# Hymba encoder: order of the fillings beside the HGRN scan

## Reference

```
h = rms_norm(x, norm1_w);  u = h @ w_in
y_a = rwkv7_mixer(shifted part of u)          # (T, 512)
y_b = hgrn2_mixer(u): chunked scan, both directions, o = o_fwd + o_bwd
      o = o * rsqrt(mean(o*o per head) + eps) * gnorm_w * silu(gate)   # (T, 512)
x  = x + concat(y_a, y_b) @ w_out
h2 = rms_norm(x, norm2_w)
group = argmax(h2 @ wg + bg); experts = top2 of 8 in the group; gates by softmax
x  = x + sum of gate * (silu(h2 @ w_gate[e]) * (h2 @ w_up[e])) @ w_down[e]
return rms_norm(x, final_norm_w)
```

## Time and profile before

| | us |
|---|---|
| median of 3 runs (2427.3 to 2428.68) | 2428.27 |
| the profiled execution, its own time | 2425.25 |
| its span, first to last instruction | 2423.6 |
| TensorE busy over the span | 2266.9 (94%) |
| VectorE / ScalarE / GpSimd busy | 1028.8 / 719.3 / 418.3 |
| 1401.6 to 1662: TensorE busy, of 260.4 | 243.15 |
| 1400 to 1410: mean granted clock | 0.73 |
| last router matmul of the stage starts | 1667.15 |
| first expert matmul starts | 1703.73 |

### The profile page before, as it was taken

How to read it: one execution, slowest core, us unless ns; L and a number is a source line. 1 busy time by engine, 2 the same in 40 slices (tenths; PEclk the granted TensorE clock), 3 DMA queues, 4 the chain that set the end, 5 groups by cost and what they waited for, 6 DMA issues and landing times. The chain is left out here.

```text
span 2423.6 us, 64805 instructions
## 1 busy us (share of the span) xinstructions
PE 2266.9 (94%) x28110; PEld 1485.1 (61%) x28110; DVE 1028.8 (42%) x2175; ACT 719.3 (30%) x1446; POOL 418.3 (17%) x520
## 2 busy tenths in 40 slices
PE   7989999989999999999968888995899999999997
PEld 4444544445555555555556656753788888888883
DVE  3236777634745645645645645543111111111115
ACT  4224554534544534534512312221000000000003
POOL 1002222200000000000012100012433334333331
PEclk9999999999999999999969988997899999999999
DMA  4113343533342432432366733251899999999986
GB/s 137 35 49 130 133 153 122 190 71 90 90 125 65 117 99 69 121 95 68 109 193 179 214 111 102 92 184 48 325 360 358 332 360 332 357 331 357 363 308 227
DMA packets 359836, 436.48 MB, mean 180 GB/s; under 512 B 164896, under 2 KB 296112, under 8 KB 351408
## 3 DMA queue, kind: packets, MB, share of 16 engines
q1 hardware_dynamic: 343232, 397.94, 48.2%
q0 software_dynamic: 14256, 35.04, 5.9%
q10 hardware_dynamic: 2112, 0.01, 0.1%
HBM read 329.87 MB, written 102.93 MB: 179 GB/s over the span
## 5 line engine op out<-in xcount | busy, mean ns | idle before, releaser
L1161 PE MATMUL h_pp<-hT,r_wcol 128*128 128x512 f32 x832 | 414.1, 621 | 9.1 <-ACT h_iraw L1289 9.1
L2715 PE MATMUL e_ps_gu<-e_xT,e_wg 128*128 128x128 f32 x2048 | 236.6, 277 | 18.3 <-DVE e_xT L2790 18.3
L2715 PEld LDWEIGHTS e_ps_gu<-e_xT,e_wg 128*128 128x128 f32 x2048 | 233.8, 194 | 18.8 <-DVE e_xT L2790 18.8
L2715 PEld LDWEIGHTS e_ps_gu<-e_xT,e_wu 128*128 128x128 f32 x2048 | 233.7, 192 | 14.8 <-issue 14.8
L2715 PE MATMUL e_ps_gu<-e_xT,e_wu 128*128 128x128 f32 x2048 | 233.9, 275 | 0.0
L2724 PE MATMUL e_ps_y<-e_wd,e_hid 128*128 128x512 f32 x512 | 225.1, 593 | 1.1 <-DVE e_hid L2804 1.1
L1161 PEld LDWEIGHTS h_pp<-hT,r_wcol 128*128 128x128 f32 x832 | 142.1, 190 | 130.2 <-issue 109.2
L500 PE MATMUL h_pp<-hT,r_wcol 128*128 128x512 f32 x480 | 209.0, 593 | 1.3 <-DVE hT L770 1.3
L2797 DVE TENSOR_SCALAR e_y<-e_ps_y,e_row 128x512 f32<-128x512 f32 x32 | 24.0, 750 | 336.0 <-PE e_ps_y L2724 336.0
L2724 PEld LDWEIGHTS e_ps_y<-e_wd,e_hid 128*128 128x128 f32 x512 | 95.0, 191 | 108.3 <-issue 108.3
L500 PEld LDWEIGHTS h_pp<-hT,r_wcol 128*128 128x128 f32 x480 | 90.3, 190 | 109.7 <-issue 108.0
(11 more groups left out here) (374 smaller groups left out, 3456.8 us busy)
## 6 DMA issues: line engine op xcount, KB each, us to landing
e_wg<-in_moe_w_gate_dram SPq DMA_DIRECT2D x32, 2048.0 KB
e_wu<-in_moe_w_up_dram SPq DMA_DIRECT2D x32, 2048.0 KB, 14.6
e_wd<-in_moe_w_down_dram SPq DMA_DIRECT2D x32, 2048.0 KB
r_wcol<-in_w_in_dram SPq DMA_DIRECT2D x35, 512.0 KB, 5.3
ar<-r_ar SPq DMA_DIRECT2D x24, 512.0 KB, 2.7
kb<-r_kb SPq DMA_DIRECT2D x24, 512.0 KB, 2.8
m_ar<-ar SPq DMA_DIRECT2D x48, 256.0 KB, 4.7
m_kb<-kb SPq DMA_DIRECT2D x48, 256.0 KB, 3.5
```

What stands on the lines that cost most here:

```text
L1161: last = nc.tensor.matmul(pp[n % 2][:], wcol[(k + 2) % 3][:, c], self.hT[:, c, span(s)], start=c == 0, stop=c == KT - 1)
L2715: last = nc.tensor.matmul(ps[:, q * P:(q + 1) * P], w[u][:, c, q * P:(q + 1) * P], xT[u][:, c * P:(c + 1) * P], start=c == 0, stop=c == KT ...
```

## The change

The earliest scan step now stands with every filling of a tile, not with those of the norm alone, and `gap` takes the first item of the list that is due, wherever it stands, passing over those that are not. `n_sq` of a tile stands one tile earlier, right behind `n_wide` of the tile before it. For the first six tiles both HGRN halves move up by one place: `half(n,0,1)` stands where `half(n,0,0)` stands for later tiles, `half(n,1,1)` where `half(n,0,1)` stood. In the loop over steps 8 and 9 the test goes by name and tile, since the item now holds its step. No instruction is added or taken away in this stage.

```
--- before.py
+++ after.py
@@ -1797,29 +1797,29 @@
 
                 def late(name, n, cost, *more):
                     if 0 <= n < TILES:
-                        out.append((name, (n,) + more, cost, 0))
+                        out.append((name, (n,) + more, cost, ready(n)))
 
                 def route(name, n, *more):
                     g = (n - 1) // 2 - 1
                     if n % 2 and 0 <= g < LAST_PAIR:
-                        out.append((name, (g,) + more, 0.4 if name == "rank" else 0, 0))
+                        out.append((name, (g,) + more, 0.4 if name == "rank" else 0, ready(2 * g + 1)))
                 norm("n_sq", 0)
                 norm("n_ss", 0, 0.9)
                 norm("n_inv", 0)
                 norm("n_wide", 0, 1.1)
+                norm("n_sq", 1)
                 for n in range(TILES + 1):
-                    norm("n_sq", n + 1)
                     late("h2n", n - 1, 0)
-                    if n >= EARLY:
-                        late("half", n, 3.5, 0, 0)
+                    late("half", n, 3.5, 0, int(n < EARLY))
                     norm("n_ss", n + 1, 0.9)
                     route("choose", n, 0)
                     late("turn", n - 1, 1.1, 0)
                     if n == TILES:
                         route("place", n - 1)
                     norm("n_inv", n + 1)
-                    late("half", n, 3.5, 0, 1)
+                    late("half", n, 3.5, int(n < EARLY), 1)
                     norm("n_wide", n + 1, 1.1)
+                    norm("n_sq", n + 2)
                     route("choose", n, 1)
                     if n >= EARLY:
                         late("half", n, 3.5, 1, 0)
@@ -1827,7 +1827,8 @@
                     if n < TILES - 1:
                         route("weigh", n)
                     late("turn", n - 1, 1.1, 1)
-                    late("half", n, 3.5, 1, 1)
+                    if n >= EARLY:
+                        late("half", n, 3.5, 1, 1)
                     late("x1", n, 0)
                     late("routed", n - 1, 1.7)
                     route("rank", n)
@@ -1849,8 +1850,8 @@
                         do[name](*args)
 
                 def gap(c, budget):
-                    while rest and budget > 0 and rest[0][3] <= c:
-                        name, args, cost, _ = rest.pop(0)
+                    while budget > 0 and any(item[3] <= c for item in rest):
+                        name, args, cost, _ = rest.pop(next(i for i, item in enumerate(rest) if item[3] <= c))
                         run(name, *args)
                         budget -= cost
                 run("r_sum", 0)
@@ -1868,7 +1869,7 @@
                 for c in range(TILES):
                     more = c + 1 < TILES
                     if TILES_P <= c < TILES_P + 2:
-                        while ("x1", (2 * (c - TILES_P) + 1,), 0, 0) in rest:
+                        while any(item[:2] == ("x1", (2 * (c - TILES_P) + 1,)) for item in rest):
                             name, args, _, _ = rest.pop(0)
                             run(name, *args)
                     budget = 2.0 if c < TILES_P // 2 + 1 else 6.0
```

## The result

The changed kernel takes 2474.63 us (median of 4 runs, 2472.55 to 2476.66), before 2427.78 (median of 4, 2426.7 to 2428.68): a ratio of 1.0192, 95% interval 1.018 to 1.0205, some 47 us slower. The forecast was 2461.8 with a range of 2447 to 2477, so the time lies in the range, near its upper end. The profiled execution of the change took 2476.66 us (span 2475.1).

A forecast was written before the change was run, and what follows sets the result against it. TensorE bounds the expert stage, which only shifts; the stage before it changes by idle +21.9, overlap +1.9, `n_ss(13)` +0.8 and clock +8.9, together +33.5 us. Forecast 2461.8 us, range 2447 to 2477.

The forecast's parts named there:

- the likeliest case: Whole kernel: the forecast's own case, 2461.8 us, 2452 to 2472 for this case alone, chance 0.66.
- rival 3: Tiles 2 to 5 and behind the stall: clock slow to come back, about 2477 us, chance 0.14.
- Idle time: TensorE from first `half` to last `rank`: 39.1 us in 24 stops against 17.2 in 12, +21.9.
- Part 1: Squares one tile ahead: made while a `half` runs, so the 12.1 us of `n_ss` waits go.
- Part 2: Tiles 0 to 5, halves ahead of `turn`: uncovered copies and `x1` cost 18.7 us against 13.9 that go.
- Part 3: Unready fillings passed over: tile 7 run out in scan step 9, waits summing to 11.0 us; tile 8 bare, 3.6.
- The clock: Lower level behind clusters of stops, 2.4 us each for most: 20.9 us against 12, +8.9.
- lost overlap: At each TensorE stop: the 0.16 us overlap of successive matmuls ends, +1.9 us in all.
- 0.8 for `n_ss(13)`: Tiles 0 and 1: `n_ss(13)` lay beside a wait before and now costs its own 0.8 us.
- Rival 1: Scan step 9: stall cheap if VectorE reaches `h2n(7)` and the choice early; about 2445 us, chance 0.13.
- Rival 2: Copies and VectorE steps run ahead everywhere, decided at `turn(2,1)`: not slower, about 2424 us, chance 0.06.

The follow-up runs named there:

- e3: Part 1 alone (squares one tile ahead) on the kernel before the change: 2425.96 us, ratio 1.0005.
- e8: Change without Part 3; in the first six tiles `routed`, `rank`, `place` behind the later tile's first half, `x1` right behind the second: 2418.95 us, ratio 0.9963.
- e9: e8 with `rank` and `place` of a pair moved behind `n_inv`, ahead of `half(n,1,1)`: 2409.93 us, ratio 0.9917.
- e5: The change, with the late fillings of tile 7 due in scan step 10 instead of 7: 2452.28 us, ratio 1.0100.
- e6: The change, with 24 unread transposes added in front of the wait of `rank(3)`: 2468.86 us, ratio 1.0154.
- e7: The change, with `weigh` one place later, behind `turn(n-1,1)`: 2476.21 us, ratio 1.0195.
- e10: e8 with Part 3 (passing over fillings not due) added: 2449.04 us, ratio 1.0077.
- e1: The change without Part 3, only a square that is not due may be passed over: 2438.79 us, ratio 1.0054 to before.

## Why the prediction was right, and where its sum was short

The direction, the mechanisms and the places were right. The size was not: the sum was 33.5 us, and the stage shows 45.2. By its own account the likeliest case reached to 2472 us, and 2474.63 lies above that, nearer to the 2477 of rival 3 (chance 0.14) than to the 2461.8 forecast. That the time fell within the stated range is owed to the width that rival 3 had added. By its steps:

- **Idle time**, +21.9 forecast, +23.8 measured. Of the stops of parts 1 and 2 each is within 0.2 us of its figure, and so are the waits at tile 8 (0.61, 1.36, 1.61, 1.41, 1.36, 0.93). The difference is the five gaps inside `scores`, 2.2 us, which I did not have.
- **Part 1.** "The 12.1 us go" was right in the change. One of the five waits, 2.04 us, was for `place` and not for squares, so it was not part 1 that took it away. e3 shows why the rest can't be booked as a gain of part 1 either: alone, three waits go to `turn` and the first stays.
- **Part 2.** The named causes hold: `half` behind `x1`, `routed` behind the copy. That it was the missing cover and not the new place of the halves is shown by e8 and e9, which keep the place and lose the waits from tile 2 on.
- **Part 3.** Right in place and size of the waits; e5 corrects the reason. I argued from tile 7 and its missing successor, but tile 6 does the same when tile 7 is held back.
- **The clock** is the step that failed, "That is 20.9 against 12: +8.9". TensorE's busy time rose by 21.4 us. With the forecast's 1.9 for lost overlap and 0.8 for `n_ss(13)` taken off, 18.7 is clock, twice the figure. Two things make the missing 10. First, I booked 2.4 us of clock behind the stall: measured, the level came back after 3 us, fell again 3.6 us later and stayed down for 10, and `grow` to `grow` took 16.3 us where e6 has 7.4 without its new wait, 8.8 more, 2.2 of them the gaps; so 6.6 for 2.4. Second, I gave a cost to the long clusters and none to waits of 1.25 (`routed(0)`: 1.0 us on itself and 2.4 on its half, 6.02 for 3.60) and 0.73 (`half(7,0,0)`: 5.37 for 3.60). These are 5.2 us more in this trace. A fixed price for a stop is itself a fault of the sum: in e5, e6 and e7 `routed(0)` waits the same 1.25, takes 1.97 or 1.98, and its half 5.38 for 6.02, and in e9 `half(7,0,0)` takes 3.67 behind the same 0.73. The trace of before had a hint of it: there a `half` ran at 5.29 behind a wait of 1.12, and I booked that under the longer one ahead of it.
- **Rivals.** The third named two causes, and one is there: the scan's short matmuls thin behind the stall, and the clock slow to come back for good. The other, clusters too close together in tiles 2 to 5, is not needed; e7 shows only that a cluster's price hardly depends on its wait. Rival 1 is refuted by the two waits in the stall, which stand in the change and again in e10. Rival 2 decided at `turn(2,1)`, and ScalarE was not ahead there.

What stays open: why 1.25 us ahead of `routed` costs slow work, and 1.22 us ahead of `turn_k` does not. None of the runs tells them apart. Open too is why the same wait, with the same work ahead of it and behind it, costs 2 us of pace in one trace and nothing in another. And it is open what the gaps in `scores` are: e6 shows that they go when TensorE is kept busy in the stall. They are not a mark of the lower level, since e5 has none at 0.50 and four of the change's five lie where the clock was back at 1.00.

## What to carry to other kernels

Count what a stop does to the pace of the work behind it, not only the stop: here the same matmuls took 21 us more for 24 us more of waiting, and shortening two waits from 3.5 to 1.25 us gave nothing in the median. A step that another engine has to answer (a copy, a choice) needs a piece of independent matmul work right behind it in the list; moving such a piece ahead of the step pays only if another takes its place, and passing over what is not due spends those pieces early. Try each part alone, and then with its cover: parts 1 and 2, which made 15 us of loss here, came with 21 us of gain after `routed`, `rank` and `place` stood behind a half and `x1` ahead of VectorE's other steps. And before a few us between two traces are explained, look at a stretch that both kernels share: here it differed by 4 us.

## What the runs showed of the hardware

- A wait of 0.73 us ahead of a half was followed by a half of 5.37 us for 3.60 in the change, e1 and e3, with the clock at its lower level in part of it. In e9 the same half behind the same wait took 3.67, with the clock at 1.00:

```profile
1519.08 3.67 PE L2154 MATMUL o_ps_out<-o_wout,y 128*128 128x512 f32 x8 [0.73 <-DVE y L2387]
```

  The Trainium skill (TensorE: Matmul & The Clock Gate, A second HAM failure mode) tells of a kernel in which short idle times between groups of matmuls sent the clock to and fro. These traces agree, and show that it does not happen at each such wait: 1.8 us of price in three of them, none in e9.
- Behind a stall with 11 us of idle time the level came back after 3 us of 128x128 and 128x32 matmuls, and fell again 3.6 us later for 10 us (the change, 1607 to 1624 us). 4 us of transposes within the stall took both away: the clock was at 1.00 from 1603 to 1614 (e6).
- Behind the stall `scores` shows gaps of 0.2 to 1.0 us between its 128x32 matmuls that no semaphore ends, most of them where the granted clock is back at 1.00 (the change, e7, e10). The same matmuls ran at 0.50 without a gap in e5, and at 1.00 without one in e6.
- The part ahead of the stage, with nearly the same instructions in the same order, ended anywhere in 19 us over thirteen traces. A profile's span can't be set against another's to better than that here; a stage's own length can, to some 4 us.
